# GpSimd adds four squared tiles in place of six in two norms, and the last activation piece of each feed-forward gets a slot of its own

## The reference

```python
def rms_norm(x, gain):
    y = xf * lax.rsqrt(jnp.mean(xf * xf, axis=-1, keepdims=True) + EPS)
    return (y * gain.astype(jnp.float32)).astype(x.dtype)
...
def swiglu(h, w_in, w_out):
    gate, up = jnp.split(h @ w_in, 2, axis=-1)
    return (jax.nn.silu(gate) * up) @ w_out
...
        x = x + g1 * o_lat
        x = x + g2 * swiglu(modulate(rms_norm(x, norm_gain[i, 1]), sh2, sc2), ffn_w_in[i], ffn_w_out[i])
```

## Time and profile before

| | |
|---|---|
| median of 3 runs | 1249.61 us (1249.21 to 1250.48) |
| the profiled execution's own time | 1249.41 us |
| its span | 1247.7 us |
| PE busy | 1187.5 us, 95% of the span |
| DVE busy | 704.2 us, 56% |
| ACT busy | 542.4 us, 43% |
| GpSimd busy | 86.4 us, 7% |
| share of PE in the chain that ended last | 82% |

### The profile page before, as it was taken

How to read it: one execution, slowest core, us unless ns; L and a number is a source line. 1 busy time by engine, 2 the same in 40 slices (tenths; PEclk the granted TensorE clock), 3 DMA queues, 4 the chain that set the end, 5 groups by cost and what they waited for, 6 DMA issues and landing times.

```text
span 1247.7 us, 18627 instructions
## 1 busy us (share of the span) xinstructions
PE 1187.5 (95%) x7096; PEld 983.6 (79%) x7096; DVE 704.2 (56%) x1174; ACT 542.4 (43%) x1002; POOL 86.4 (7%) x124
## 2 busy tenths in 40 slices
PE   7999999999999999899989989999989999999898
PEld 5765787787788887578965889999979885998466
DVE  3544576767623334667679564445576465445753
ACT  3234422222222323544358554445455675565752
POOL 0002011122100000100000200000010000200400
PEclk9999999999999999899999999999999999999999
DMA  9889455677632233122330245555535341653110
GB/s 327 305 304 324 138 164 174 201 265 247 231 101 76 94 101 101 35 100 74 130 102 1 70 156 180 188 182 171 174 102 160 130 135 35 155 174 135 35 65 37
DMA packets 121510, 183.32 MB, mean 147 GB/s; under 512 B 4321, under 2 KB 92688, under 8 KB 121440
## 3 DMA queue, kind: packets, MB, share of 16 engines
q1 hardware_dynamic: 113888, 154.64, 37.1%
q0 software_dynamic: 7552, 27.73, 7.1%
HBM read 181.31 MB, written 1.05 MB: 146 GB/s over the span
## 4 chain that ended last, share of the span: by engine, by line
PE 82%; DVE 8%; ACT 4%; issue 3%; POOL 1%; DMA 0%; DVEq 0%; SPq 0%; ACTq 0%; POOLq 0%
PE ps L464 20%; PE ps L466 20%; PE ps L465 20%; PE ps L794 2%; PE ps L796 2%; PE ps L795 2%; PE ps L835 2%; PE ps L2097 1%; PE ps L2141 1%; PE ps L2429 1%; PE ps L2431 1%; PE ps L2430 1%; PE ps L1274 1%; ACT wh L442 1%; DVE wl L449 1%
## 5 line engine op out<-in xcount | busy, mean ns | idle before, releaser
L449 DVE TENSOR_TENSOR wl<-raw,wh 128x1024 fp32r<-128x1024 f32 (+1 forms) x246 | 295.4, 1206 | 248.2 <-ACT wh L442 245.3
L464 PE MATMUL ps<-hh,wh 128*128 128x256 f32 (+2 forms) x1256 | 419.6, 334 | 13.5 <-DVE hl L594 8.3
L465 PE MATMUL ps<-hl,wh 128*128 128x256 f32 (+2 forms) x1256 | 410.3, 327 | 0.0
L466 PE MATMUL ps<-hh,wl 128*128 128x256 f32 (+2 forms) x1256 | 409.3, 326 | 0.0
L442 ACT ACTIVATE wh<-raw 128x1024 fp32r<-128x1024 f32 (+1 forms) x246 | 252.4, 1031 | 274.5 <-PE ps L466 256.2
L464 PEld LDWEIGHTS ps<-hh,wh 128*128 128x128 f32 x1256 | 238.1, 190 | 54.8 <-issue 24.8
L465 PEld LDWEIGHTS ps<-hl,wh 128*128 128x128 f32 x1256 | 237.5, 189 | 22.2 <-issue 1.9
L466 PEld LDWEIGHTS ps<-hh,wl 128*128 128x128 f32 x1256 | 238.3, 190 | 20.9
L464 PE MATMUL ps<-ah,wh 128*128 128x256 f32 (+2 forms) x392 | 131.9, 336 | 3.7 <-DVE al L1927 3.0
L465 PE MATMUL ps<-al,wh 128*128 128x256 f32 (+2 forms) x392 | 129.6, 331 | 0.0
L466 PE MATMUL ps<-ah,wl 128*128 128x256 f32 (+2 forms) x392 | 129.5, 330 | 0.0
(11 more groups left out here) (224 smaller groups left out, 1424.0 us busy)
## 6 DMA issues: line engine op xcount, KB each, us to landing
raw<-in_ffn_w_in SPq DMA_DIRECT2D x44, 1024.0 KB, 5.1
raw<-in_ffn_w_out SPq DMA_DIRECT2D x22, 1024.0 KB, 4.9
raw<-in_w_in SPq DMA_DIRECT2D x22, 1024.0 KB, 5.4
big<-in_w_ada SPq DMA_DIRECT2D x16, 1024.0 KB, 9.4
big<-in_w_ada POOLq DMA_DIRECT2D x24, 512.0 KB, 4.4
ex<-in_w_ada POOLq DMA_DIRECT2D x24, 512.0 KB, 4.9
raw<-in_diff_w_in SPq DMA_DIRECT2D x12, 1024.0 KB, 5.1
raw<-in_w_out SPq DMA_DIRECT2D x8, 1024.0 KB, 4.9
```

Of the source, the lines that this page charges most:

```text
L449: ins = nc.vector.tensor_tensor(place(wl), v, place(wh).bitcast(F32), ALU.subtract)
L464: nc.tensor.matmul(o, w_hi, m_hi, start=first, stop=False, **kw)
L465: nc.tensor.matmul(o, w_hi, m_lo, start=False, stop=False, **kw)
L466: return nc.tensor.matmul(o, w_lo, m_hi, start=False, stop=last, **kw)
```

## The change

`GATHERED` now gives a number of tiles for each norm: six as before in "ffn0" and "diff", four in "ffn1" and "second". There GpSimd makes three adds in place of five, and PE sums tiles 4 and 5 one by one as well. The squares of tiles 6 and 7 then wait for PE's sums of tiles 4 and 5.

In both feed-forwards piece 21 is rounded to `hh[:, 0]` and split to `hl[:, 0]`. These hold the input of the feed-forward's first half, which has been used up by then. Its rounding stands directly behind that of piece 20, ahead of the two weight halves.

```diff
--- before.py
+++ after.py
@@ -510,13 +510,16 @@
         SUMS = {"ffn0": [(5, 0, NT)], "diff": [(0, 0, NT)], "ffn1": [(7, 0, L)],
                 "second": [(0, 0, L2)], "lat": [(7, 0, L), (6, L, HW)]}
 
-        GATHERED = ["ffn0", "diff", "ffn1", "second"]
-        N_ADDED = KD - 2
+        GATHERED = {"ffn0": KD - 2, "diff": KD - 2, "ffn1": KD - 4, "second": KD - 4}
         sq_acc = big[:, 13312:13824]
 
         def added_before(name, k):
 
-            return GATHERED.index(name) * (N_ADDED - 1) + max(k, 0)
+            base = 0
+            for other, added in GATHERED.items():
+                if other == name:
+                    return base + max(k, 0)
+                base += added - 1
 
         def norm_square(act, name, k):
 
@@ -524,7 +527,7 @@
             b = BASE[name]
             if name in X_OF:
                 act.wait_ge(s_x, X_OF[name] + k + 1)
-            if name in GATHERED and k >= 2:
+            if k >= 2 and name in GATHERED and k - 2 < GATHERED[name]:
                 act.wait_ge(s_added, added_before(name, max(k - 2, 1)))
             elif k >= 2:
                 act.wait_ge(s_sum, b + k - 1)
@@ -606,7 +609,7 @@
         def squares_added(pool, name):
 
             n = sum(p[2] for p in NORMS[name][2])
-            for k in range(1, N_ADDED):
+            for k in range(1, GATHERED[name]):
                 pool.wait_ge(s_sq, BASE[name] + k + 1)
                 if k == 1:
                     positive(pool, s_sum, BASE[name])
@@ -618,12 +621,12 @@
         def norm_sum(pe, name, k):
 
             tiles, _, parts, _, _ = NORMS[name]
-            if name in GATHERED and k < N_ADDED:
-                if k == N_ADDED - 1:
+            if name in GATHERED and k < GATHERED[name]:
+                if k == GATHERED[name] - 1:
                     pe.wait_ge(s_added, added_before(name, k))
                     bank, a, b = SUMS[name][0]
                     nc.tensor.matmul(ps[:, bank, 0:b - a], T["ones"], sq_acc[:, a:b], start=True, stop=False)\
-                        .then_inc(s_sum, N_ADDED)
+                        .then_inc(s_sum, GATHERED[name])
                 return
             pe.wait_ge(s_sq, BASE[name] + k + 1)
             for bank, a, b in SUMS[name]:
@@ -1654,8 +1657,9 @@
                         act_round(layer, i * 8 + (j + 4), j, n, q0)
                         round_half(act, i * 8 + (q0 + 2 + j + AHEAD), q0 + 2 + j + AHEAD)
                 act.wait_ge(s_act, (layer + 1) * KF)
+                act_round(layer, 20, 20, n, q0)
+                nc.scalar.activation(hh[:, 0, 0:n], big[:, 21 * n:22 * n], ACT.Copy).then_inc(s_ar, 1)
                 for k in range(18, 20):
-                    act_round(layer, k + 2, k, n, q0)
                     round_next(act, q0 + k)
                 for m in range(KD):
                     norm_square(act, norm, m)
@@ -1941,8 +1945,11 @@
                     for j in range(8):
                         act_split(layer, i * 8 + (j + 4), j, n, q0)
                         split_low(dve, i * 8 + (q0 + 2 + j + AHEAD), q0 + 2 + j + AHEAD)
+                act_split(layer, 20, 20, n, q0)
+                dve.wait_ge(s_ar, (layer + 1) * KF)
+                nc.vector.tensor_tensor(hl[:, 0, 0:n], big[:, 21 * n:22 * n], hh[:, 0, 0:n].bitcast(F32),
+                                        ALU.subtract).then_inc(s_as, 1)
                 for k in range(18, 20):
-                    act_split(layer, k + 2, k, n, q0)
                     split_next(dve, q0 + k)
                 for m in range(KD):
                     if m < KD - 1:
@@ -2305,8 +2312,9 @@
                     c = slice(m * P, (m + 1) * P)
                     for k in (20, 21):
                         at = (q0 + k) % SPLIT_SLOTS
-                        ins = product(ps[:, m, 0:n], wh[:, at, c], wl[:, at, c], ah[:, k % 2, 0:n],
-                                      al[:, k % 2, 0:n], False, k == 21)
+                        high, low = (ah[:, 0, 0:n], al[:, 0, 0:n]) if k == 20 else \
+                            (hh[:, 0, 0:n], hl[:, 0, 0:n])
+                        ins = product(ps[:, m, 0:n], wh[:, at, c], wl[:, at, c], high, low, False, k == 21)
                     if m < KD - 1:
                         ins.then_inc(s_fin, 1)
                     else:
```

## The result

The changed kernel takes 1253.83 us (median of 7 runs, 1251.16 to 1254.49) where the kernel before takes 1249.61 (7 runs, 1248.91 to 1251.44). The ratio is 1.0024, its 95% interval 1.0013 to 1.0034: slower, by a quarter of a per cent. On a second chip the same kernel stood at 1252.61 (10 runs) against 1250.16 (27 runs), ratio 1.0018 (1.0009 to 1.0028). The forecast was 1248.4, in a range of 1247.2 to 1250.1.

The account below looks back on a forecast made before the run. PE, at work for 95% of the span, was taken to bound the kernel. -1.55 + 0.86 - 0.45 = -1.15 us gave 1248.3 from the profiled execution, 1248.5 from the median; 1248.4 was taken, range 1247.2 to 1250.1.

Parts of the forecast that it names:

- Where PE waits: Whole kernel: PE works 95% of the span, so time changes only where PE waits or gets more to do.
- shifts are carried one for one: Stretches the diff touches: no transfer ends a PE wait there, so any shift reaches the program's end in full.
- Term 1: End of the first feed-forward: piece 21's own slot removes PE's wait, -1.55 us, bounds 0 to -1.7.
- Term 2: Norm "ffn1": two more sums on PE between products, +0.86 us, bounds 0.7 to 1.1.
- Term 3: End of the second feed-forward, slot and sums together: stall moves ahead of two tiles, -0.45 us, bounds -1.04 to +1.2.
- Rival A: Second feed-forward's end: PE's clock falls in the moved stall, 1.7 us lost, 1250.0 us; chance 0.22.
- Rival C: Both feed-forwards: DVE's split or the adds' pace eats the slot's gain, likelier half of it, 1249.5 us; chance 0.10.
- the sign: First feed-forward: sum over 13.3 us after the first of the last products would show the slot's gain eaten; 13.0 was due.
- Rival D: Behind the other two norms: low-clock stretches turn out longer or shorter, 0.8 us each side; chance 0.60 shared with the sum.
- Rival B: Second feed-forward's end: PE's 2.05 us wait for GpSimd simply goes, -3.0 us in all, 1246.4; chance 0.08.

Follow-up runs that it names:

- filling: Products of ones that nobody reads, put into PE's idle time at the norms; kernel before 0.9996, slot in both feed-forwards with six tiles 0.9966, twice.
- before_fill: Kernel before plus products of ones at three norms ("diff" 5 ahead, 16 behind the sums; "second" 8 ahead; "ffn1" 11 behind): 1249.13 us, ratio 0.9996.
- slot_only: Changed kernel with six tiles added on GpSimd in all norms, keeping piece 21's own slot: 1250.87 and 1250.63 us, ratios to before 1.0000 and 1.0005.
- the delayed ones: 6 or 12 products of ones delaying the later stages: on the kernel before 1251.76 and 1254.13 us, on the slot with six tiles 1251.80 and 1252.10.

## Why the prediction was wrong

**Where PE waits, and that shifts are carried one for one.** The first half was right. The second, "what is shifted there is carried to the end of the program one for one", failed: without filling nothing of the slot's shift arrived at the end (ratios 1.0000 and 1.0005), with the clock held up at the norms 2.8 us did.

**Term 1, the slot in the first feed-forward, -1.55.** Measured 1.49 in the first profile. The part on what is late next (DVE's split before the first update, level again at tile 1) is in the rows. What was missed: with the earlier wait gone, the wait for GpSimd grows from 1.47 to 1.94 us and the clock then falls ahead of or in the norm's own sums in 6 of 11 profiles, which takes up to 1.7 us back.

**Term 2, the norm "ffn1", +0.86.** Measured 0.85, no new wait.

**Term 3, both edits at the end of the second feed-forward, -0.45.** Measured -0.13. The place and size of the stall (2.1 forecast, 1.93 measured) and the time of the logarithm (0.1 off) were right. Two sizes were off. DVE's split of a weight half, started when ACT has rounded it behind square 7, ends after the exponential and holds the first scaled tile back by 0.2 to 0.3 us: I had looked at ACT and PE as ends of the path and not at DVE. And the slot alone gives 1.4 us there where the clock stays up (14.82 to 13.43 in the table), not 1.04; 0.4 of it is what the profile of before has over before_fill (14.40), which has no fall at 918.7. Against that the sums cost 1.26 there and not 0.59.

**Rival A, the clock in the new stall.** It did not happen in any of the four profiles that have this stall unfilled. The mechanism was the right one at the wrong place: it came in "diff", and in "second" where six tiles are kept.

**Rival C, the slot gives nothing.** That is what slot_only measured, with a chance of 0.10, but not by the cause named: the sum of "diff" starts 13.05 us after the first of the last products (502.71 - 489.66), where 13.0 was due and 13.3 was the sign.

**Rival D, the clock behind the norms as a spread of 0.8 us to each side.** This is the step that failed. It took the low stretches as luck that evens out over executions, looked for them behind two norms only, and left 0.04 for a time over 1252.1. They do not even out: the mean granted clock goes from 0.991 to 0.9885 and 0.9893 with the slot, some 5 to 7 us more at the lower level. The extra stretches lie over the sums of "diff" and of "second", behind "ffn1", and in the second attention, which the prediction did not look at.

**The balance.** An estimate from the profiles with the slot and no filling in the stage, each stage's mean length against before: -0.62 us in (a), +0.52 in (b), -0.69 in (c) and +1.35 in (d), together +0.6 ((b) and (d) without the delayed ones). Without the clock it would have been -1.5 and -1.4, so the clock took some 3.5. The slot measured +0.83 and +0.86 by the medians of two chips, +0.1 and +0.6 by the means. The sums measured +2.1 without the slot, with the slot 0.85 and 1.26 by their rows. Together that is 2.7 to 3.0 us; measured +4.2 and +2.5 by the medians, +3.1 and +2.5 by the means. **Rival B** did not come about: the adds were not ahead. The Trainium skill's advice against GpSimd for such adds (GPSIMD Engine Reference, section "Engine selection") did not help here: in "ffn1" PE did not wait for them, and in "second" its wait was merely moved up. Its ratio to VectorE is not tested, since no run put these adds there.

**What stays open.** That the clock takes the slot's gain is shown by the filling. Why the second attention, with no instruction changed, has 6.8 to 10.2 us at the lower level in 11 of 12 profiles of slot kernels without filling and 3.4 in three of the four without the slot, is not: the delays give no clear answer, and the filled kernels have 6.8 there too. Nor is it shown why the wait of 1.9 us is followed by a fall in one execution and not in the next.

## What to carry to other kernels

Before taking out a wait of PE, look at the waits behind it and at PE's clock there: here the slot's 1.5 and 1.4 us were there only in the profiles in which the clock stayed up over the sums behind it. Where PE must wait at a norm, a few products that nobody reads, as many as fit, kept its clock up. Neither alone was clear of noise in this kernel (slot 1.0000 and 1.0005, filling 0.9996), and both together gave 0.9966, twice. A wait that is moved is not removed: ahead of the last two tiles PE's wait for GpSimd was still 1.93 us, and with the two sums more the end came 1.3 us later. And a profile of one execution cannot show a loss that lies in how often the clock falls, so compare the mean granted clock over executions as well.

## What was not expected of the hardware

The granted clock fell after a wait of only 1.91 us that PE's sums followed at once (0.53 from 501.4 us on), though not in every execution. The mean granted clock of a kernel moved by 0.002 to 0.003 with an edit that leaves the number and shape of PE's products as they were. And the second attention took 60.0 to 62.5 us in kernels in which no instruction of it differs.
